# Routing and the experts' start in a one-core decoder block: operand halves inside the choice, last tile's turn and logits, job table, zeroing and load order

## What is computed

```python
h = h + merged @ w_out[l]
hn = rmsnorm(h, norm2_g[l])
g_logits = hn @ w_group + b_group;  g_idx = argmax(g_logits)        # group
e_logits = (hn @ w_router + b_router)[g_idx]                        # its 8 experts
top_l, top_i = top_k(e_logits, 2);  w = softmax(top_l) * g_w
y = sum over both: w * ((silu(hn @ w_gate[e]) * (hn @ w_up[e])) @ w_down[e])
```

## Time and profile before

| | us |
|---|---|
| median of 3 runs (lowest, highest) | 2815.13 (2812.27, 2816.78) |
| the profiled execution's own time | 2826.66 |
| its span in the trace | 2825.0 |
| PE busy in the span | 2515.1 (89%) |
| DVE busy | 1755.8 (62%) |
| ACT busy | 1048.6 (37%) |

### The profile page before, as it was taken

How to read it: one execution, slowest core, us unless ns; L and a number is a source line. 1 busy time by engine, 2 the same in 40 slices (tenths; PEclk the granted TensorE clock), 3 DMA queues, 4 the chain that set the end, 5 groups by cost and what they waited for, 6 DMA issues and landing times. The chain is left out here.

```text
span 2825.0 us, 36971 instructions
## 1 busy us (share of the span) xinstructions
PE 2515.1 (89%) x12303; PEld 2017.3 (71%) x12303; DVE 1755.8 (62%) x2528; ACT 1048.6 (37%) x1524; POOL 566.6 (20%) x502
## 2 busy tenths in 40 slices
PE   4999999999899899999929998886499989999986
PEld 3898888999878798898916776665366666666652
DVE  6599997776120288888835554555466666666641
ACT  4201001443221287787821113222344444444430
POOL 3132222111111011111110010021323333333321
PEclk9999999999999999999969998998699999999998
DMA  5121212233214424345057646334388989899983
GB/s 128 46 67 54 74 52 83 75 113 113 87 65 132 125 81 107 92 126 147 16 150 198 181 142 233 122 134 164 112 342 338 351 333 354 339 342 345 351 314 136
DMA packets 181933, 477.69 MB, mean 169 GB/s; under 512 B 33292, under 2 KB 104076, under 8 KB 147372
## 3 DMA queue, kind: packets, MB, share of 16 engines
q1 hardware_dynamic: 132658, 370.45, 39.0%
q0 software_dynamic: 33264, 58.98, 6.2%
q10 hardware_dynamic: 15890, 46.67, 4.3%
HBM read 415.40 MB, written 117.21 MB: 189 GB/s over the span
## 5 line engine op out<-in xcount | busy, mean ns | idle before, releaser
L92 PE MATMUL project_bank<-project_xnT_hi,project_w_hi 128*128 128x512 f32 (+4 forms) x1352 | 511.2, 378 | 1.3 <-DVE project_xnT_lo L667 0.7
L93 PE MATMUL project_bank<-project_xnT_lo,project_w_hi 128*128 128x512 f32 (+4 forms) x1352 | 498.9, 369 | 0.0
L94 PE MATMUL project_bank<-project_xnT_hi,project_w_lo 128*128 128x512 f32 (+4 forms) x1352 | 496.7, 367 | 0.0
L717 DVE SCALAR_TENSOR_TENSOR project_work<-project_work,project_taps 128x2048 f32<-128x2048 f32 x128 | 335.5, 2621 | 4.5
L2404 DVE TENSOR_TENSOR experts_gu_lo<-weights_gate_up,experts_gu_hi 128x2048 fp32r<-128x2048 f32 x128 | 288.0, 2289 | 62.3 <-ACT experts_gu_hi L2346 61.9
L2346 ACT ACTIVATE experts_gu_hi<-weights_gate_up 128x2048 fp32r<-128x2048 f32 x128 | 244.3, 1911 | 163.7 <-DMA weights_gate_up<-in_w_up_dram 136.6
L2308 PE MATMUL experts_y_bank<-weights_down,experts_hT 128*128 128x512 f32 x544 | 256.9, 616 | 27.3 <-issue 26.3
L92 PEld LDWEIGHTS project_bank<-project_xnT_hi,project_w_hi 128*128 128x128 f32 (+1 forms) x1352 | 251.4, 186 | 36.9 <-issue 8.5
L93 PEld LDWEIGHTS project_bank<-project_xnT_lo,project_w_hi 128*128 128x128 f32 (+1 forms) x1352 | 251.2, 186 | 33.2 <-issue 6.8
L94 PEld LDWEIGHTS project_bank<-project_xnT_hi,project_w_lo 128*128 128x128 f32 (+1 forms) x1352 | 251.5, 186 | 27.2 <-issue 0.6
L1088 DVE TENSOR_TENSOR attend_pT<-attend_t_bank,attend_pT 128x512 fp32r<-128x512 f32 (+3 forms) x352 | 214.2, 615 | 23.7 <-ACT attend_pT L1038 22.7
(11 more groups left out here) (264 smaller groups left out, 4482.9 us busy)
## 6 DMA issues: line engine op xcount, KB each, us to landing
weights_gate_up<-in_w_gate_dram SPq DMA_DIRECT2D x68, 1024.0 KB
weights_gate_up<-in_w_up_dram SPq DMA_DIRECT2D x68, 1024.0 KB
weights_down<-in_w_down_dram SPq DMA_DIRECT2D x68, 1024.0 KB
project_w_raw<-in_w_in_dram SPq DMA_DIRECT2D x36, 512.0 KB, 4.1
qk_d<-project_work SPq DMA_DIRECT2D x16, 1032.0 KB, 5.4
gate_d<-project_work ACTq DMA_DIRECT2D x16, 1024.0 KB, 4.2
merge_gates<-gate_d SPq DMA_DIRECT2D x16, 1024.0 KB, 5.5
first_half<-qk_d SPq DMA_DIRECT2D x24, 512.0 KB, 15.7
```

Of the source, the lines that this page charges most:

```text
L92: pe.matmul(out, lhs[0], rhs[0], start=first, stop=False)
L93: pe.matmul(out, lhs[0], rhs[1], start=False, stop=False)
L94: return pe.matmul(out, lhs[1], rhs[0], start=False, stop=last)
L717: nc.vector.scalar_tensor_tensor(out=work[:, 2, 0:SEQ], in0=work[:, 1, META - 1 + q:META - 1 + q + SEQ], scalar=taps[:, bass.ds(ct, 1), q] ...
```

## The change

- `over_chunks` loses its loop: all four chunks are straight code on all engines, and so are SP's loads and POOL's scatters.
- The halves of tile 3 of chunks 1 to 3 move. ACT's `high_m` comes ahead of its wait for the exponentials; DVE's `low_m` goes into `choose`, after its eighth step.
- The last tile's turn (n = 15) goes to `h_bank[:, 0]` instead of `t_bank` (`turned`), and no longer waits for `hn_lo_ready`.
- The last chunk's logits are made in two halves of 256 columns: that of tiles 12 and 13 before the turn of tile 15, the other behind it. The first writes where the ranks of chunk 2 are, so DVE's reading of them is cut out of `find_slots` as `take_ranks`, stands right behind the sum of tile 15, and PE waits for it (`slot_step`). The rest of `find_slots(2)` moves behind `lower` of tile 15.
- POOL scatters all four k = 0 first, once slots of k = 0 are there, then k = 1.
- The three job columns are one transfer of 32 rows of three; the readers' addresses change from j + 32 k to 3 j + k.
- Experts: `rows` is zeroed by DVE ahead of its wait for the table, `sofar` by POOL behind the first two gathers, and SP waits for the rows of job 0 before it loads gate and up for job 2.

```diff
-            for j in range(CHUNK):
-                tile(0, j)
...
-            with eng.Fori(1, NC - 1) as c:
-                chunk(c)
-            chunk(NC - 1)
+            for c in range(NC):
                 for j in range(CHUNK):
                     tile(c, j)
-                    tail(c - 1, j, False)
+                    if c:
+                        tail(c - 1, j, False)
...
+            def logits(c, first, end):
+                pe.wait_ge(hn_lo_ready, c * CHUNK + (end + 1))
...
+                    if last:
+                        pe.wait_ge(slot_step, (c - 1) * 5 + 1)
+                        logits(c, 0, CHUNK // 2)
                     turn(c, CHUNK - 1)
                 elif part == 1 and not behind:
...
+                    logits(c, CHUNK // 2 if last else 0, CHUNK).then_inc(logits_done, 1)
...
                 elif part == 1:
+                    if c < NC - 1:
+                        high_m(c + 1, CHUNK - 1)
                     wait(act, choice_step, c * STEPS + EXP_STEP)
...
                 step(v.tensor_reduce(e(2), p64.rearrange("p t (g j) -> p t j g", j=PER_GROUP), AX.X, ALU.add))
+                if c < NC - 1:
+                    low_m(c + 1, CHUNK - 1)
...
+                if n == NT - 1:
+                    take_ranks(NC - 2)
...
-                wait(pool, slots_ready, c * 4 + 4)
-                for j in range(CHUNK):
-                    for k in range(2):
+                for k in range(2):
+                    wait(pool, slots_ready, c * 4 + (3 + k))
+                    for j in range(CHUNK):
...
+            wait(sp, rows_loaded[0], 16)
             load_gate_up(2, 0, expert_of(2))
...
-            chain(nc.gpsimd.memset(rows[:, :, :], 0.0), 3)
-            chain(nc.gpsimd.memset(sofar[:, :, :], 0.0), 4)
-            pool.sem_inc(y_free, 2)
...
+            wait(pool, rows_zeroed, 1)
             gather(0, 0)
             gather(1, 1)
+            chain(nc.gpsimd.memset(sofar[:, :, :], 0.0), 3)
+            pool.sem_inc(y_free, 2)
...
+            nc.vector.memset(rows[:, :, :], 0.0).then_inc(rows_zeroed, 1)
```

More of the change, by code:

```diff
@@ L1564, in stage_route, with turned, over_chunks @@
         hn_tiles = hn_d.rearrange("(t p) d -> t p d", p=P)
-        def over_chunks(eng, tile, tail, after):
-            for j in range(CHUNK):
-                tile(0, j)
-                if j:
-                    after(0, j - 1)
-            def chunk(c):
+        def turned(n):
+            return t_bank if n < NT - 1 else h_bank[:, n % 2 ^ 1]
+        def over_chunks(tile, tail, after):
+            for c in range(NC):
                 for j in range(CHUNK):
                     tile(c, j)
-                    tail(c - 1, j, False)
+                    if c:
+                        tail(c - 1, j, False)
                     if j:
                         after(c, j - 1)
-                    tail(c - 1, j, True)
-            with eng.Fori(1, NC - 1) as c:
-                chunk(c)
-            chunk(NC - 1)
+                    if c:
+                        tail(c - 1, j, True)
             for j in range(CHUNK):
@@ L1611, in _ @@
             sp.dma_start(table_d.rearrange("(p n) o -> p (n o)", p=P), empty).then_inc(table_cleared, 16)
-            with sp.Fori(1, NT // 2) as it:
-                for b in range(2):
-                    load_tile(it * 2 + b, b)
+            for n in range(2, NT):
+                load_tile(n, n % 2)
             wait(sp, w_ready, DC + 1)
@@ L1660, in scatter @@
                 pool.sem_inc(slots_free, 1)
-            with pool.Fori(0, NC) as c:
+            for c in range(NC):
                 scatter(c)
@@ L1716, in tail @@
                     m.then_inc(rank_done, 1)
-            over_chunks(pe, tile, tail, turn)
+            over_chunks(tile, tail, turn)
             pe.wait_ge(final_step, 1)
@@ L1779, in tail @@
                     nc.scalar.activation(small[:, 6, :], small[:, 5, :], ACT.Exp).then_inc(exp_ready, 1)
-            over_chunks(act, tile, tail, high)
+            over_chunks(tile, tail, high)
             wait(act, final_step, 17)
             act.dma_start(jobs_d[:, 0:1], job_count[:, :]).then_inc(final_stored, 16)
-            for k in range(3):
-                act.dma_start(jobs_d[:, 1 + MORE_JOBS * k:1 + MORE_JOBS * (k + 1)].rearrange("o j -> j o"),
-                              job[:, k:k + 1], allow_slow_non_contiguous=True).then_inc(final_stored, 16)
-            wait(act, final_stored, 64)
+            act.dma_start(jobs_d[:, 1:1 + 3 * MORE_JOBS].rearrange("o (j k) -> (o j) k", k=3),
+                          job[:, 0:3], allow_slow_non_contiguous=True).then_inc(final_stored, 16)
+            wait(act, final_stored, 32)
         @block.vector
@@ L1820, in tile @@
                 s = stat[:, b, :]
[L1821 removed]
+                if j == CHUNK - 1:
+                    if c < NC - 1:
+                        low_m(c + 1, 0)
+                elif j < CHUNK - 2 or c == 0:
                     low_m(c, j + 1)
[L1823 to L1824 removed]
                 wait(dve, x_loaded[b], c * 32 + (16 * (j // 2) + 16))
@@ L1940, in tail @@
                     lower(c, CHUNK - 1)
+                    if c == NC - 1:
+                        find_slots(c - 1)
                 elif part == 1 and behind:
                     choose(c)
-                elif part == 3 and behind:
+                elif part == 3 and behind and c != NC - 2:
+                    take_ranks(c)
                     find_slots(c)
@@ L1949, in _ @@
             wait(dve, tiled, CHUNK)
-            over_chunks(dve, tile, tail, lower)
+            over_chunks(tile, tail, lower)
             v = nc.vector
```

50 lines of the change are left out of this document (26 added, 24 removed).

## The result

| | before | changed |
|---|---|---|
| median, us (lowest, highest) | 2813.70 (2811.84, 2816.78), 4 runs | 2773.14 (2771.47, 2780.55), 4 runs |
| the same in a second session | 2814.50 (2812.36, 2822.05), 9 runs | 2773.29 (2768.52, 2774.45), 5 runs |
| ratio, with its 95% interval | | 0.986 (0.9839, 0.9881); second 0.9845 (0.983, 0.9861) |
| the profiled execution, and its span | 2826.66, 2825.0 | 2771.47, 2769.8 |

A forecast was written before the change was run, and what follows sets the result against it. PE bounds route, losing time to low-half waits; engine chains bound route's end and experts' start. Terms 20.4 + 3.3 + 3.7 + 1.0 + 6.8 = 35.2 us off 2815.13 gave 2780 us, range 2773 to 2791.

The forecast's parts named there:

- job table: End of route: job transfers are covered by the scatters up to 1990.5, so the single transfer gains nothing.
- waits for the low half: Route: all five PE waits for the low half of the merged values go, 14.6 us.
- transposes of the logits: Route, looped chunks: PE's wait falls from 1.46 to the straight chunk's 0.86 us, 1.2 us in all.
- Part 1: Route's chunks: halves inside the choice and straight code remove PE's waits and the lower clock after them, 20.4 us.
- Part 2: Route's last tile: its turn in its own bank gains 3.3 us, the last logits in halves 3.7 us.
- Part 3: End of route: scatters start with k = 0, whose slots are ready earlier, 1.0 us; nothing from the job transfers.
- Part 4: Start of experts: earlier first gather, landing 3 us after it is out because SP waits for the rows; 6.8 us.
- Rival 1: Start of experts: both subtractions hold the gather, weights delay the second; gain only 1.6 us, time 2785; chance 0.12.
- Rival 2: Route: a new PE stall per chunk, at tile 2's turn or the chunk's start; time 2790; chance 0.09.
- Rival 3: End of route: POOL's chunk 2 scatters bound the last slots, 2 us lost, time 2782; chance 0.06.
- Rival 4: Route: tile 3's high half waits for its load, DVE stops inside the choice; 20.4 becomes about 5, 2795; chance 0.03.
- Rival 5: Experts' loop: the start shifts its phase, gathers fall behind weight loads, kernel slower, 2831 at 0.8 us a job; chance 0.03.

The follow-up runs named there:

- job3: Changed kernel, but the job columns are three transfers again instead of one; 2778.22 us, one run.
- no_exp: Changed kernel with the old start of experts: POOL zeroes both buffers before the gathers, SP doesn't wait for rows; 2778.92 us, ratio 0.9873 to before.
- sp_free: Changed kernel without SP's wait for the rows of job 0 before job 2's gate and up load; 2774.33 us, one run.
- dve_yields: Changed kernel, but DVE begins its first two weight subtractions only when POOL has issued both first gathers; 2771.09 us, ratio 0.9838 to before.

## Why the prediction was right, and where it was not

The forecast was 35.2 us less, and 40.6 were measured; the traces of the first pair have 41.0 in the stages that the change touches. The time of 2773.1 us is inside the stated range by 0.1 only, and outside the 2774 to 2786 to which the forecast gave 0.67. Of the 6.8 us between it and the 2779.9 of the sum, 5.4 are gain that the sum didn't have, and 1.4 come from the median of before, which was 2815.13 when the forecast was made and 2813.70 with a fourth run. That it fell inside owes something to luck: most steps were right, but the largest error, the job table, had no place in the range. Step by step, as forecast and as read from the distances:

| step | forecast | measured |
|---|---|---|
| waits for the low half | 14.6 | 15.9 |
| clock after long waits | 4.6 | 4.2 |
| transposes of the logits | 1.2 | 2.7 |
| last turn in its own bank | 3.3 | 3.3 |
| logits in halves | 3.7 | 3.6 |
| scatters, k = 0 first | 1.0 | 1.5 |
| job table | 0 | 3.6 |
| start of experts | 6.8 | 6.2 |
| sum | 35.2 | 41.0 |

**Part 1.** The size was nearly right, 22.8 for 20.4 (the first three lines are the differences between PE's intervals in the two kernels). A wait costs a little more than its idle time in the row: behind 5.62 us idle PE's first matmul began 6.65 us after the turn, and 0.79 in the changed kernel, 5.9 more. The transposes were sized by the straight chunk of before, 0.86 us of idle time; in the changed kernel it was 0.32 to 0.40 in all three. Why the straight chunk of before had more was not shown. What the forecast did not do is to divide the 14.6 us. It named both causes, the slow looped choice and the place of the half, and credited them together. The runs divide them: 19.2 to the straight code, 3.5 to the place, and of the loop nearly all to DVE. Whoever had only moved the operand halves into the choice, the change that the title names first, and kept the loop would have got 3.7 us.

The cover that the forecast called thin held: PE didn't wait for turned rows between tile 0 and tile 14 in any kernel with a straight choice. With the looped one it was gone, and PE lost 5.7 and 5.5 us at exactly that place.

**Part 2.** Both terms came out right to 0.1 us, the second by luck. Its 24 matmuls took 4.5 us at a mean clock of 0.62 (columns as in the earlier trace rows). The forecast had twelve at 0.24 us and twelve at 0.14; it was about sixteen at 0.21 and eight at 0.12, and the two errors cancel. In job3, where all 24 ran at 0.50, they took 5.2. (Two products of the forecast are also rounded down: 24 × 0.12 is 2.9, and its 4.5 is 4.56. Neither moves the sum by more than 0.1.)

```profile
1933.50:1938.00 4.50, 4.47 (x24) 0.62 0.01 0
```

**Part 3.** The step that failed is "the job transfers left from 1983.6 on and are covered by the scatters up to 1990.5". Their issue was covered, their landing was not: the stage ended 14.7 us behind the first of them. The sign was in the rows, a gap of 7.8 us behind the last scatter, with no engine busy, and no sentence of the forecast explained that gap. It also means that the 1.0 us of the scatters' order would have been nothing without the single transfer. The remaining 0.5 of the scatters is POOL's own loop, which the forecast didn't count.

**Part 4.** The first gather ended 0.9 us behind the first subtraction, as forecast from the earlier trace rows, and its rows took 3.2 us, as forecast from the earlier trace rows. It was out 6.2 us behind the stage's start instead of 5.6, since the subtractions began 3.0 us into the stage and not 2.4: that is the 0.6 us of difference. DVE's memset ended at 2.9, and the table may have held them too: in no_exp, without this memset, it reached DVE only at 3.0. The reason given for the 3 us was wrong in one point. SP's wait does not protect the first gather, which is out before the weights in any case; it protects the second.

**Rivals.** Rival 1 didn't come: the second turn stood 4.4 us behind the first, as PE needs it, and 2.7 later without SP's wait. Rival 2 didn't either, there was no new stall. Rival 3: POOL ended its scatters of chunk 2 at 1945.0, and DVE began the slots of chunk 3 at 1949.6 with no wait for it. Rival 4: DVE had no wait at the low half inside the choice. Rival 5: the kernel was not slower, but the distance from PE's first turn to the end was 794.9 and not 811. By the forecast's own words that was to be a sign of something wrong. What was off was the reference: the second trace of before has 801.9, and the medians differ by no more than the stages explain. What made the first trace of before 9 us longer there stays open.

## What to carry to other kernels

A chain of small dependent instructions is where straight code pays: here a third of the time from step to step was the loop's, and it cost 18 us in 8 tiles of a stage where PE was otherwise full. Before a gain is put down to the new place of an instruction, ask what the waiting engine will wait for next: with the low half moved and the loop kept, PE's wait of 5.6 us for the low half came back as one of 5.7 us for the turned rows. At the end of a stage look for a gap with no engine busy, find the transfer that lands in it, and count a small transfer until it has landed, not until it is issued.

## What the runs showed of the hardware

- A DVE step of 0.19 us that waits for the one before starts 0.22 to 0.23 us after it in straight code and 0.33 to 0.34 us in a hardware loop whose waits compare with a register and are followed by an increment. POOL's scatter began 0.44 us after the start of the DVE step it waits for in straight code, and 0.98 in the loop.
- One transfer of a single value and three of 32 single values each, started by ACT over 1.8 us, held the end of a stage until 13.9 to 14.7 us after the first was started. With one transfer of 32 rows of three in place of the three, both were down within 9.4. Whether the number of transfers or the single values make the difference was not separated.
- PE could use the rows of an indirect gather of 128 rows 3.2 to 3.4 us after POOL had it out when that was ahead of the loads of 2 MB of weights (by 1.3 us in sp_free, and with SP waiting for the rows elsewhere), and 7.7 to 8.2 us after when it was 0.9 behind their start.
- An indirect transfer started while DVE subtracts two operands in SBUF ended 0.9 us behind that subtraction: at the start of experts in before, the changed kernel, no_exp, sp_free and dve_yields, and in all 66 cases between 2100 and 2300 us of before, the changed kernel, no_exp and dve_yields. Without a subtraction it takes 1.0 us.
